# Products with ones in the RMS norms: one moving column instead of 128

## What is computed

```
def rms_norm(x, g):
    xf = x.astype(jnp.float32)
    y = xf * lax.rsqrt(jnp.mean(xf * xf, axis=-1, keepdims=True) + NORM_EPS)
    return (y * g.astype(jnp.float32)).astype(x.dtype)

x = x + rms_norm(mix, g[1])
f, fb = conv_ffn(rms_norm(x, g[2]), ...)
x = x + rms_norm(f, g[3])
```

## Time and profile before

| | |
|---|---|
| median of three executions | 3577.77 us |
| the profiled execution, its time | 3572.24 us |
| its span, first to last instruction | 3570.5 us |
| mean granted TensorE clock | 0.965 |
| TensorE busy (matmul) | 3318.4 us, 93% |
| VectorE busy | 1872.5 us, 52% |
| ScalarE busy | 1169.2 us, 33% |
| matmuls of `sums`, L1089 | 648 records, 78.5 us busy |

### The profile page before, as it was taken

The page is one execution under the profiler, slowest core; times in us unless marked ns, Lnnn a source line. Parts: engine busy times, 40 slices in busy tenths (PEclk is TensorE's granted clock), DMA queues, the critical chain, the costliest instruction groups (busy, mean ns, idle before and its releaser), DMA issues. The chain is left out here.

```text
span 3570.5 us, 53355 instructions
## 1 busy us (share of the span) xinstructions
PE 3318.4 (93%) x20054; PEld 3152.5 (88%) x20054; DVE 1872.5 (52%) x2806; ACT 1169.2 (33%) x1907; POOL 519.3 (15%) x789
## 2 busy tenths in 40 slices
PE   4548999999999998999988999979999999999997
PEld 4448999999999998999986799979999999999997
DVE  7943554554444546322236666644655545455456
ACT  5232444322333223322245322224443222222222
POOL 2241001000010012000012333310001000000011
PEclk7678999999999999999999999999999999999999
DMA  3445541111111113332349522224544343443443
GB/s 85 128 115 138 163 131 42 42 43 42 42 42 42 42 53 113 108 113 97 112 139 329 181 83 83 83 83 136 161 134 128 118 133 114 130 127 119 131 133 127
DMA packets 398386, 389.53 MB, mean 109 GB/s; under 512 B 45652, under 2 KB 336792, under 8 KB 398040
## 3 DMA queue, kind: packets, MB, share of 16 engines
q1 hardware_dynamic: 372666, 324.06, 29.7%
q0 software_dynamic: 18336, 55.14, 4.7%
q10 hardware_dynamic: 7176, 7.35, 0.7%
HBM read 281.45 MB, written 102.63 MB: 108 GB/s over the span
## 5 line engine op out<-in xcount | busy, mean ns | idle before, releaser
L1242 PE MATMUL pair<-x_head,w_head 128*128 128x384 f32 x2544 | 863.2, 339 | 55.5 <-DVE w_rest L841 31.2
L1242 PE MATMUL pair<-x_rest,w_head 128*128 128x384 f32 x2544 | 855.4, 336 | 0.0
L1242 PE MATMUL pair<-x_head,w_rest 128*128 128x384 f32 x2544 | 855.3, 336 | 0.0
L1532 DVE SCALAR_TENSOR_TENSOR cv<-u,par,cv 128x1024 f32<-128x1024 f32 x176 | 225.5, 1281 | 663.9 <-ACT u L1473 663.9
L841 DVE TENSOR_TENSOR w_rest<-w_raw,w_head 128x1024 fp32r<-128x1024 f32 x260 | 317.5, 1221 | 460.6 <-ACT w_head L837 460.5
L1242 PEld LDWEIGHTS pair<-x_head,w_head 128*128 128x128 f32 x2544 | 481.5, 189 | 76.5 <-issue 59.2
L1242 PEld LDWEIGHTS pair<-x_rest,w_head 128*128 128x128 f32 x2544 | 481.7, 189 | 0.0
L1242 PEld LDWEIGHTS pair<-x_head,w_rest 128*128 128x128 f32 x2544 | 481.3, 189 | 0.0
L837 ACT ACTIVATE w_head<-w_raw 128x1024 fp32r<-128x1024 f32 x260 | 275.9, 1061 | 580.3 <-PE pair L1434 280.6
L1468 ACT ACTIVATE cv<-pair,par 128x384 f32<-128x384 f32 x264 | 177.0, 670 | 615.7 <-PE pair L1242 602.5
L1434 PE MATMUL pair<-a_head,w_head 128*128 128x384 f32 x1056 | 361.4, 342 | 5.2 <-DVE f L1565 3.7
(11 more groups left out here) (487 smaller groups left out, 5004.5 us busy)
## 6 DMA issues: line engine op xcount, KB each, us to landing
w_raw<-in_ffn_w_up_dram SPq DMA_DIRECT2D x88, 512.0 KB, 4.1
hs<-in_state_mlstm_C_dram SPq DMA_DIRECT2D x32, 1024.0 KB, 9.0
c_room<-in_state_mlstm_C_dram SPq DMA_DIRECT2D x64, 512.0 KB, 5.6
out_dram<-c_room SPq DMA_DIRECT2D x64, 512.0 KB, 4.6
w_raw<-in_s_w_glu_dram SPq DMA_DIRECT2D x48, 512.0 KB, 4.2
w_raw<-in_mlstm_w_down_dram SPq DMA_DIRECT2D x48, 512.0 KB, 4.1
w_raw<-in_ffn_w_down_dram SPq DMA_DIRECT2D x44, 512.0 KB, 3.7
w_raw<-in_mlstm_w_up_dram SPq DMA_DIRECT2D x32, 512.0 KB, 4.7
```

What stands on the lines that cost most here:

```text
L1242: m = pe.matmul(out[:, 0:TB], lhs[slot][:, P * k:P * k + P], rhs[:, k, TB * c:TB * c + TB], start=(k == 0 and q == 0), stop=(k == KD - 1 a ...
L1532: ins = dve.scalar_tensor_tensor(out=cp, in0=up[:, j:j + SEQ], scalar=tw, in1=cp, op0=ALU.mult, op1=ALU.add)
```

## The change

In `sums` the moving operand becomes the first column of `ones`, and the result one column of bank 6 in place of 128. The stationary operands, the number of matmuls, their order, the semaphores and the three columns that `roots` reads stay as they are.

```
@@ -1086,7 +1086,7 @@
                 pe.wait_ge(self.rooted, g)
             for h in range(2):
                 for j in range(self.TT):
-                    m = pe.matmul(self.env.bank[6][:, P * j:P * j + P], self.slot(g, k)[:, h, P * j:P * j + P], self.env.ones[:, :],
+                    m = pe.matmul(self.env.bank[6][:, P * j:P * j + 1], self.slot(g, k)[:, h, P * j:P * j + P], self.env.ones[:, 0:1],
                                   start=(k == 0 and h == 0 and j == 0), stop=(k == parts[-1] and h == 1), skip_group_check=True)
             m.then_inc(self.summed, 1)
```

## The result

| | before | after |
|---|---|---|
| median of four executions | 3576.19 us (3574.26 to 3582.33) | 3609.49 us (3607.04 to 3610.09) |
| ratio, 95% interval | | 1.0093 (1.008 to 1.0106) |
| profiled execution: time, span | 3572.24, 3570.5 us | 3609.93, 3608.2 us |
| mean granted TensorE clock | 0.965 | 0.950 |

A forecast was written before the change was run, and what follows sets the result against it. TensorE, busy 93% of the span, was taken as the bound. Clock losses of 17.0 + 9.1 + 6.0 + 4.0, less 2.6 and 4 us cover, gave 29.5 us, rounded to 29; forecast 3606 us, range 3589 to 3621.

The forecast's parts named there:

- The price of a narrow record is the weight load's: In the sums, records with one moving column come every 106 ns, the pace of loading 128 x 128 weights.
- the 2.6 us that I credited: Over all 648 records of the sums, 106 ns each in place of 110: 2.6 us saved.
- Streams of 5 us lose the clock, those of 1.3 us keep it: Each of eleven long groups of sums (5.1 us narrow) drops TensorE's clock to half; ten gathered groups (1.3 us) do not.
- A step of 6.8 us behind each, half of it lost: Each fall of TensorE's clock lasts 6.8 us at half, 3.4 us of work lost.
- the forecast's 36.1 us: Clock losses at the eleven long groups: 17.0 + 9.1 + 6.0 + 4.0 us, before credit and cover.
- The pair: Two successive long groups at 1387.8, 10.2 us of narrow work: 18.2 us at half clock, 9.1 us lost.
- the five groups between products: Long groups with products right before and behind (507.9, 1344.4, 1358.3, 1368.2, 2622.1): 5 x 3.4 = 17.0 us lost.
- the three with a wait: Long groups before TensorE's wait for scale and split (526.4, 1414.6, 2640.7): clock falls earlier, 2.0 us each, 6.0 us lost.
- Cover of 4 us: TensorE's waits, for `w_rest` and steps begun earlier, take up 4 us of the delay.
- That the clock doesn't fall: Rival: TensorE keeps full clock through the narrow sums, only the 2.6 us count, 3575 us; chance 0.07.
- That short records are faster: Rival: one-column records of the sums take 66 ns, 28 us saved, 3549 us; chance 0.03.
- That the delay is swallowed: Rival: clock falls, but waits behind the groups absorb most delay; 13 us stay, 3591 us; chance 0.07.

The follow-up runs named there:

- the best kernel here: Squares and ones of the sums in reduced f32, 128 moving columns, orientation and root as before, against the kernel before the change: 3555.31 us, ratio 0.9934.

## Why the prediction was right, by its steps

- *The price of a narrow record is the weight load's.* Right, and shown by 64 moving columns at the same pace and by 64 stationary columns at about half of it. But the 2.6 us that I credited for 106 in place of 110 ns aren't there. Both figures are lengths of a group shared out over its records, and hold the changeover at its ends. Between the second and the last record of a group the starts are 111 or 112 ns apart with 128, 64, 32 and 1 columns alike, and so they are in the stream of 8 columns in the earlier trace rows. From a gathered group's start to the next product it is 1.25 us before and 1.26 after.
- *Streams of 5 us lose the clock, those of 1.3 us keep it.* Right at all eleven long groups and nine of ten gathered ones. The tenth, late and already at half clock, delays the return by 3.4 us; I had looked only at what lowers the clock, not at what raises it. That a short narrow stream passes was read from two places, of 1.7 and 2.9 us, and is no rule: with two columns in reduced f32 the clock fell 2.4 us after the start of one group and right behind another of 2.7.
- *A step of 6.8 us behind each, half of it lost.* The stretches were too short in the forecast and the loss in them too large. In the kernel after, the stretches at half in or behind the groups add up to 129.7 us (twelve, from 3.4 to 17.1), with TensorE busy in 109.7 of them; before, to 30.7 (five), busy in 22.5. That is 87 us more of work at half, where the forecast's 36.1 us meant 72. The pair fits: 17.1 us at half, forecast 18.2. Of the five groups between products, two have 10.2 us and not 6.8; behind the three with a wait the fall is 13.7 to 17.1 us, where 6.8 and some 4 more were expected. On the other side, half clock doesn't double every time: in these traces records of the sums start 213 ns apart in place of 112, and products of 384 columns 320 in place of 173 or 174. So a microsecond of work at half is 0.46 to 0.48 lost, and 87 us about 40.
- *Cover of 4 us.* Nearly right: in the four stages TensorE is idle 2.5 us less. The delay of the sums moves the chain behind them along, as the prediction said. The 20 us that TensorE stands still in the longer stretches at half (129.7 less 109.7) are no cover; they are waits that happen to lie there and cost nothing at either clock.
- The sum: 36.1 - 2.6 - 4 = 29.5 us were forecast, and 38.4 - 2.5 = 35.9 measured in the four stages. The credit that wasn't there and the falls that were longer make most of the difference. By stage, with the cover and before the credit, 5.4, 17.3, 5.4 and 4.0 us were forecast; 6.2, 19.0, 6.5 and 4.2 were measured. That the time came out within 3.5 us, 3606 against 3609.5, is in part luck: the forecast was a rise of 28 us from a median of 3577.8, and the rise was 33 from 3576.2.
- *The rivals.* That the clock doesn't fall is refuted by the trace; that its fall has another cause, by the pair of runs with 64 and 32 columns. That short records are faster is refuted by the pace, the same with 64 columns as with 128. That the delay is swallowed is refuted too: 2.5 us of 38.4 were.
- A reading that was inexact: the control isn't "twice 5.3 us" at the pair but 5.96 and 5.43 us, with 0.44 us of idle in the first.

The reading of the Trainium skill that a gapless stream keeps the clock ("TensorE: Matmul & The Clock Gate", Part 1: The HAM clock gate) is contradicted by the kernel after: from 507.46 to 518.6 TensorE is never idle and is at half from 511.8. Its price for a load, columns over 1.2 GHz (same page, LDWEIGHTS), would be 107 and 53 ns; between starts the traces show 112 and 58.

## What to carry to other kernels

When each matmul brings its own full stationary operand, count the loads, not the moving columns: from 128 columns down, cutting columns saved nothing here, and cutting loads (one record in place of two) did. Columns that look wasted may be what holds the clock for the large products behind them; before narrowing a stream of several us, look for a narrow stream in the trace and read the granted clock behind it. Time that TensorE saves can also go to the clock: in the best kernel here nearly half of it did, so compare the work done at half clock before and after, not the busy time alone. Price a new operation in the chain by its own duration, the reciprocal on 384 values above all, before counting what it replaces.

## What the runs showed of the hardware that I had not expected

- Narrow records also delay the clock's return: 10.2 us at half in place of 6.8 around a group of 12 that began at half clock, in all five traces with 1 or 32 columns there and in none of the five with 64 or 128 (sums in f32, as before). In reduced f32, where the group has 6 records, it was 6.8 us with 2 columns as with 128.
- A stream of 3.5 us with 12 + 36 narrow records was enough for a fall of 3.4 us behind it, and one of 2.7 us with 24 records of two columns in reduced f32 as well. With 128 columns, neither the group nor what followed it lost the clock at these places.
- VectorE's reciprocal of 128 x 384 values takes 2.55 us, of 128 x 3 values 0.17 us.
- Half clock costs less than a factor of two: 320 in place of 173 or 174 ns from one product of 384 columns to the next.
